# Six loads of a hybrid decoder layer's last stage, requested from ScalarE's queue in place of SyncE's

## The reference

```python
ya = _rglru_branch(xa, ...) * jax.nn.silu(ga)
yb = _dsa_branch(q, ckv, qi, ki, wi, ...) * jax.nn.silu(gb)
y = jnp.concatenate([ya, yb], axis=-1)
x = x + jnp.einsum('bse,ed->bsd', y, w_out[l])      # output projection, residual
return _rmsnorm(x, final_norm_g)                    # x * rsqrt(mean(x*x) + eps) * g
```

## Time and profile before

| | us |
|---|---|
| median of three runs | 1460.89 |
| the profiled execution | 1460.7 |
| its span in the trace | 1458.9 |
| PE busy in the span | 1437.3 (99%) |
| DVE busy | 1071.4 (73%) |
| ACT busy | 638.4 (44%) |
| POOL busy | 755.0 (52%) |

### The profile page before, as it was taken

The page is one execution under the profiler, slowest core; times in us unless marked ns, Lnnn a source line. Parts: engine busy times, 40 slices in busy tenths (PEclk is TensorE's granted clock), DMA queues, the critical chain, the costliest instruction groups (busy, mean ns, idle before and its releaser), DMA issues.

```text
span 1458.9 us, 21797 instructions
## 1 busy us (share of the span) xinstructions
PE 1437.3 (99%) x7320; PEld 1278.2 (88%) x7320; DVE 1071.4 (73%) x1704; ACT 638.4 (44%) x921; POOL 755.0 (52%) x637
## 2 busy tenths in 40 slices
PE   8999999999999999999999999999999999999997
PEld 7899999988888888888888888888998888888886
DVE  6478666688789888887854566647878791899957
ACT  7345555543544534542211111145556543453564
POOL 5364454458788898885444444310000254556581
PEclk9999999999999999999999999999999999999999
DMA  8212111144545555545631333244442553344377
GB/s 287 87 51 80 44 50 43 29 137 150 164 142 182 183 177 164 163 151 193 210 124 51 94 94 96 68 171 143 147 156 93 174 171 103 102 165 153 102 232 279
DMA packets 181958, 197.15 MB, mean 135 GB/s; under 512 B 14614, under 2 KB 144776, under 8 KB 180872
## 3 DMA queue, kind: packets, MB, share of 16 engines
q1 hardware_dynamic: 180360, 192.16, 41.5%
q0 software_dynamic: 1536, 4.20, 0.8%
HBM read 141.26 MB, written 55.05 MB: 135 GB/s over the span
## 4 chain that ended last, share of the span: by engine, by line
PE 90%; DVE 5%; ACT 1%; DMA 1%; issue 1%; POOL 0%; SPq 0%; ACTq 0%; DVEq 0%
PE ps L1380 18%; PE ps L1381 18%; PE ps L1382 18%; PE ps L1629 5%; PE ps L1631 5%; PE ps L1630 5%; PE ps L1619 4%; PE ps L1600 2%; PE ps L1500 2%; PE ps L1502 2%; PE ps L1594 1%; PE ps L1593 1%; PE ps L1592 1%; PE ps L1392 1%; DVE rt L2155 1%
## 5 line engine op out<-in xcount | busy, mean ns | idle before, releaser
L1380 PE MATMUL ps<-hT_hi,w_lo 128*128 128x512 f32 (+1 forms) x1344 | 496.4, 369 | 0.0
L1382 PE MATMUL ps<-hT_hi,w_hi 128*128 128x512 f32 (+1 forms) x1344 | 495.8, 369 | 0.0
L1381 PE MATMUL ps<-hT_lo,w_hi 128*128 128x512 f32 (+1 forms) x1344 | 495.8, 369 | 0.0
L965 POOL TENSOR_TENSOR w_lo<-w_raw,w_hi 128x512 fp32r<-128x512 f32 x168 | 225.1, 1340 | 346.9 <-ACT w_hi L1050 346.8
L1380 PEld LDWEIGHTS ps<-hT_hi,w_lo 128*128 128x128 f32 x1344 | 254.1, 189 | 29.9
L1381 PEld LDWEIGHTS ps<-hT_lo,w_hi 128*128 128x128 f32 x1344 | 254.1, 189 | 29.6
L1382 PEld LDWEIGHTS ps<-hT_hi,w_hi 128*128 128x128 f32 x1344 | 254.0, 189 | 29.2
L1050 ACT ACTIVATE w_hi<-w_raw 128x512 fp32r<-128x512 f32 x168 | 104.6, 627 | 372.1 <-PE ps L1382 304.6
L994 POOL TENSOR_TENSOR wo_lo<-wo_raw,wo_hi 128x512 fp32r<-128x512 f32 x104 | 154.1, 1484 | 110.9 <-ACT wo_hi L1254 110.9
L954 POOL TENSOR_TENSOR w_raw<-w_raw,g_col 128x512 f32<-128x512 f32 x168 | 204.1, 1225 | 7.0 <-DMA w_raw<-in_w_in 7.0
L1896 DVE MATCH_REPLACE8 scores<-top,scores 128x384 f32<-128x384 f32 (+2 forms) x192 | 165.8, 876 | 0.0
(11 more groups left out here) (242 smaller groups left out, 2199.1 us busy)
## 6 DMA issues: line engine op xcount, KB each, us to landing
w_raw<-in_w_in SPq DMA_DIRECT2D x168, 256.0 KB, 2.8
tw<-in_w_out SPq DMA_DIRECT2D x128, 128.0 KB, 2.6
t_dram<-tw SPq DMA_DIRECT2D x128, 128.0 KB, 2.7
wo_raw<-t_dram SPq DMA_DIRECT2D x64, 256.0 KB, 2.6
wo_raw<-in_w_out SPq DMA_DIRECT2D x48, 256.0 KB, 3.2
xin<-in_x SPq DMA_DIRECT2D x8, 1024.0 KB, 6.9
rt<-in_x SPq DMA_DIRECT2D x10, 512.0 KB, 5.4
out<-rt SPq DMA_DIRECT2D x10, 512.0 KB, 4.2
```

The lines of the kernel that those rows point to most:

```text
L965: nc.gpsimd.tensor_tensor(w_lo[:, j, :, :], w_raw[:, j, :, :], w_hi[:, j, :, :].bitcast(F32), ALU.subtract).then_inc(w_lo_s, 1)
L1380: nc.tensor.matmul(o, wlo, hi, start=(kt == 0), stop=False)
L1381: nc.tensor.matmul(o, whi, lo, start=False, stop=False)
L1382: return nc.tensor.matmul(o, whi, hi, start=False, stop=(kt == KT - 1))
```

## The change

Four requests for x12 and two for g0 and g1 leave SP's program, where they stood between requests for weight pieces of chunk 12, and stand in ACT's program: x12's behind the roundings of pieces 4 to 7 of chunk 11, the weights' behind those of pieces 0 and 1 of chunk 12. The wait for s_lo moves with the first of them. Sizes, sources, places and semaphores of the six transfers stay.

```diff
                     sp.wait_ge(o_sq, 1 + 8)
                     for q in range(NQ):
                         sp.dma_start(r_one[q][:, :], x[rows(NQ + q), right]).then_inc(x22_in, 16)
-                if c == 12 and m < NQ:
-                    if m == 0:
-                        sp.wait_ge(s_lo, 4 * KH)
-                    sp.dma_start(x12[m], x[rows(m), right].rearrange("p (k e) -> p k e", k=2)).then_inc(x12_in, 16)
-                if (c, m) in ((12, 4), (12, 5)):
-                    part, half = ((g0, left), (g1, right))[m - 4]
-                    sp.dma_start(part[:, :], a["final_norm_g"][half].rearrange("(o d) -> o d", o=1).broadcast_to(
-                        [P, NHALF])).then_inc(gf_in, 16)
             for q in range(NQ):
                 sp.dma_start(c11_back[q], c11_d[q].rearrange("p (k e) -> p k e", k=2)).then_inc(c11_moved, 16)
```

```diff
                 out_high(c, m)
                 if c == LASTC:
                     continue
+                if c == 11 and m >= NQ:
+                    q = m - NQ
+                    if q == 0:
+                        act.wait_ge(s_lo, 4 * KH)
+                    nc.scalar.dma_start(x12[q], x[q * P:(q + 1) * P, NHALF:D].rearrange("p (k e) -> p k e", k=2)
+                                        ).then_inc(x12_in, 16)
+                if (c, m) in ((12, 0), (12, 1)):
+                    part, at = ((g0, 0), (g1, NHALF))[m]
+                    nc.scalar.dma_start(part[:, :], a["final_norm_g"][at:at + NHALF].rearrange(
+                        "(o d) -> o d", o=1).broadcast_to([P, NHALF])).then_inc(gf_in, 16)
                 if m >= 5 and c - 1 in S_AFTER:
                     i, m0 = S_AFTER[c - 1]
                     high_s(i, m0 + m - 5)
```

## The result

The changed kernel takes 1464.38 us (median of 14 runs, 1462.26 to 1466.27), the kernel before, run beside it, 1460.84 us. The ratio is 1.0021 (95% interval 1.0014 to 1.0028), so it is 2.0 to 4.1 us slower. Forecast were 1458.9 us and a range up to 1461.5 us: wrong, on the other side. The profiled execution of the changed kernel has a span of 1462.2 us against 1458.9.

A forecast was written before the change was run, and what follows sets the result against it. The last 40 us were taken as bound by DVE, with 1.7 us of waiting for a residual tile. A gain of 2.0 us from 1460.7 gave 1458.7, plus 0.19 for the median: 1458.9 us, range 1457.2 to 1461.5.

The forecast's parts named there:

- What bounds the kernel: Last 40 us: DVE's work, not PE's; DVE waits 1.7 us for a residual tile, then alternates with POOL at 2.22 us.
- upper bound: DVE's residual adds: if the first finds POOL idle, it takes 1.2 us and DVE gains 2.7 us; 2.0 taken.
- The price on ACT: Issuing six requests on ACT: 0.43 us each, costing nothing; at 1.22 us each PE comes about 1 us late.
- slower rival: ACT stands at each request until data has gone out: 1463.4 us at 2.0 us each, 1475 at 5; chance 0.12.
- SP without the six: Residual moves to a stretch with emptier DMA engines, so pieces land sooner; PE's 1.3 us stall shrinks by 0.3 us.
- room of 2.7 us: Between (11,7)'s low part ending at 1400.63 us and PE beginning it about 1403.3 us, for three ACT requests.
- The end: Last adds of row block 3: the gain is the smaller of DVE's 2.0 us and PE's 1.88 + 0.3 = 2.2 us.
- POOL pays: Earlier DVE stretches POOL's low parts, delaying PE by 1.1 us; 1460.1 us; chance 0.18 together with nothing happening.
- PE moves too: Emptier DMA engines remove PE's whole 1.3 us stall and DVE gains 3 us: 1457.7 us or less; chance 0.15.
- It does nothing: The tile lands no earlier because ACT's and SP's queues share engines worse: 1460.9 us; chance 0.18 together with POOL pays.

The follow-up runs named there:

- e7: Kernel before, with each residual tile requested on SP as soon as its own place is free, one at a time; -2.2 us against before (-3.5 to -0.9).
- e10: Kernel before, with all four residual tiles requested on SP one behind another, right after piece (13,1); +4.7 us against before (3.1 to 6.3).
- e9: Kernel before, with all six requests on ACT, the residual tiles spread early, each once its place is free; -1.8 us against before (-3.1 to -0.4).

## Why the prediction was wrong

*What bounds the kernel* was right: DVE's chain, its 1.7 us of wait, and the turns of DVE and POOL. e7 shows it: with the tile in time, DVE gains 2.5 us (forecast 2.0, between 1.7 and 2.7) and the tail 2.2 us, which is PE's bound in the forecast. Its first residual instruction found POOL idle and took 1.2 us, as the upper bound had it.

*The price on ACT* was right as far as it went: the requests took 0.35 to 0.45 us, beside the rounding, and held nobody. The slower rival, an ACT held by its requests, did not happen. The time came out on its side, by another mechanism.

*SP without the six* is the step that failed: "2 MB of the residual move into the emptier stretch [...] So pieces of chunk 12 and 13 land sooner". They landed later. I had read a mean share of 0.47 as room. The mean does not decide: with the tiles in it, that stretch has a share of 0.51 in the changed kernel, and the one in which e7 asks for its tiles has 0.54, where PE lost nothing (columns as above):

```profile
1369.00:1389.00 20.00, 20.00 (x95) 17.50 (x94) 19.70 (x23) 10.09 (x18) 10.61 (x8) 1.00 0.54 175
```

What decides is how much is in flight beside a piece. The pieces that e7 requested from 1388.7 to 1392.2 us, around one tile, landed like this:

```profile
DMA to landing us min/median/max: 2.7/3.4/3.6
```

In the changed kernel the first two tiles were requested 1.7 us apart, and the pieces requested from 1393.1 to 1395.6 us, beside both, took 5.5 to 6.1 us; in e10, behind four tiles, 8.0 to 8.2 us. And the pieces have little lead. The estimate that was missing can be made from rows of before: in chunks 11 and 12 three pieces pass through the buffers while PE does the 24 matmuls of two of them, 24 x 0.216 = 5.2 us, so four buffers turn over in 6.9 us; rounding (0.9) and low part (1.3) leave 4.7 us for landing, 3.7 where POOL's low part takes 2.25 us. In before five pieces in a row were above that or at it (4.7 to 6.3 us, requested from 1399.0 to 1406.0 us); in the changed kernel eight of nine were, in the whole stretch (4.8 to 7.1 us). Lead was lost in the first half of the move, and the second half, the weights 7.3 and 3.5 us earlier, met the last two tiles when none was left. The room of 2.7 us, which the text gives to (11,7), was set against ACT's issuing alone and not against the landing of the pieces.

*The end* was right as a bound (the smaller of DVE's gain and PE's), but PE's side was put at a gain of 0.3 us, with bounds of 0 and 1.3: no loss was allowed for. It was a loss of 5.2 us, of which 1.7 us were the lower clock after a single long stop, a term that the sum does not have.

*POOL pays* came true in part, behind the late pieces: the low part of (12,2), done before DVE's residual adds in the kernel before, fell beside them, and some 1.6 us of the stop of 3.2 us are its and (13,4)'s turns with DVE. In e7 and e9, where DVE begins no later and the pieces are on time, PE has no such stop. *PE moves too* did not happen: PE's wait of 1.3 us ahead of (12,6) stayed in all the kernels that gained, even with the bytes away. That it belongs to the turns of POOL and DVE was not tried.

*It does nothing* was set aside for 5.7 us of head start; for the tile that DVE waits for, the forecast's own moments give 1403.63 - 1399.3 = 4.3 us at most, and the run 2.8 us (requested at 1400.8 us). It was enough: the tile landed at 1407.8 us.

## What to carry to other kernels

A load that is moved earlier is paid for by whatever streams at that moment: set the landing time of the stream, beside as many such loads as will be in flight at once, against its buffers' turnover, and not the mean share of the DMA engines against 1. Which queue asks made no difference where the tiles went out one at a time; asking so, as soon as a tile's own place is free, was the gain. Where a matrix engine at full speed loses its lead, count the time at the lower clock behind the stop as well as the stop.

## What was not expected of the hardware

In e9 ACT's first request took 2.76 us, seven times the 0.37 to 0.38 us of the other three of its kind, and ACT's next rounding began 2.76 + 0.1 us behind its start, some 0.6 us later than in the kernel before (1369.69 us), where it waited for PE; in the changed kernel the first request took 0.45 us. Why is open.

```profile
1367.48 2.76 ACTq L1320 DMA_DIRECT2D plain_lo<-in_x  x1
1370.35 0.91 ACT L1246 ACTIVATE wo_hi<-wo_raw 128x512 fp32r<-128x512 f32 x1 [2.29 <-PE ps L1644]
1372.38 0.38 ACTq L1320 DMA_DIRECT2D plain_lo<-in_x  x1
```

There the 2.76 us cost nothing in the tail; what they would cost 24 us later, where (11,4) to (11,7) are rounded, was not tried.
